# The last down matrix of a decoder step in two column halves, with residual rows added on TensorE

## The chip, the cores and the metric

The kernel runs on one core of a Trainium2 chip. The metric is the device time of one execution in microseconds. A core has TensorE (matrix products into PSUM), VectorE, ScalarE, GpSimd, SyncE (which issues DMAs here) and 16 DMA engines. A DMA can also be issued by ScalarE or GpSimd; the issue then stands in that engine's own queue of instructions.

## What is computed

One decoder layer for 256 prompt tokens and 8 x 4 sample tokens, all with the same weights in float32. The change lies in the last sub-layer, the mixture of experts, and in its last expert:

```python
def hier_moe(n, w_group, b_group, w_router, b_router, w_gate, w_up, w_down):
    ...
    y = jnp.zeros_like(xf)
    for e in range(N_EXPERTS):
        h = jax.nn.silu(xf @ w_gate[e]) * (xf @ w_up[e])
        y = y + combine[:, e:e + 1] * (h @ w_down[e])
    return y.reshape(B, T, D)
...
    return h + hier_moe(rms_norm(h, norm_ffn), ...)
```

D_MODEL is 2048, EXPERT_FF 512, there are 16 experts, and a token goes to two of them. The model's y is h (the residual rows) plus the experts' weighted rows.

## The kernel before

Tokens are sorted to experts by their number. The first ten experts in that order have a block of 64 rows each, the star expert a block and a strip, and the last five (light ones) strips of 32 rows; two strips of different experts share a block. Should more tokens come to an expert than fit, up to 8 overflow blocks follow in a loop that runs none when there is no overflow (`nov` is 0).

For each expert SyncE streams six lots of 2 MB in the order gate 0, up 0, gate 1, up 1, down 0, down 1 into eight buffers in a ring; a lot waits until the one that held its buffer is used up (`moe_free`). A down lot holds, for each of 128 partitions p, the rows 4p+2q and 4p+2q+1 of the down matrix with all their 2048 columns: one piece of 16 KB per partition.

TensorE does for a light expert: gate and up (`light_gate_up`, `strip_products`, L1275: four matmuls 128x256 side by side in four column strips of the array, first half with lots 0 and 1, second half with lots 2 and 3), then ScalarE's silu (L1890), VectorE's product with up (L2430), a transposition on TensorE (L1320) that ScalarE lays into `hTs` (L1869), then the down products (`light_down`, `strip_down`, L1327): a column strip c of the array computes columns 512c to 512c+511 into PSUM partitions 32c to 32c+31. VectorE and ScalarE copy two strips each into `ysb` (`strip_rows`, L2398 and L1875). In `ysb` the partitions 0 to 63 hold the block's 64 rows with columns 0 to 1023, the partitions 64 to 127 the same rows with columns 1024 to 2047.

Combining multiplies `slot_w` (which row of the block goes to which token, with its weight) by `ysb`. For tokens t (0 and 1: the prompt's 256, 2: the 32 of the sample) and x (0 or 1) a step has two products, one on partitions 0 to 63 for columns 512x and one on partitions 64 to 127 for columns 1024+512x. VectorE adds the PSUM rows to `hx`, which holds the residual rows (L2351, L2354). For earlier blocks these steps lie between the gate products of the next expert (`between`).

At the end, after both down lots of expert 15 (`y_last`), the copies, then four steps `last_combine` (L1335) into all eight PSUM banks, VectorE's six additions (L2465), for the sample tokens four more small products (L1473) once the first addition has freed two banks, and after each addition a store from SyncE (L548). The span ends when all six have landed.

Each matmul in float32 stands in the trace as two records.

## Time and profile before

| what | us |
|---|---|
| median of 3 runs | 1251.08 |
| lowest and highest | 1248.23, 1257.48 |
| the profiled execution | 1253.98 |
| its span on the core | 1252.2 |
| TensorE busy in the span | 1165.5 |
| VectorE busy | 471.4 |
| ScalarE busy | 192.7 |

The profiled execution's own time has 1.8 us around its span. "Busy" is an average over the whole kernel. PE is TensorE's matmul, PEld its weight load, DVE is VectorE, ACT is ScalarE, SP is SyncE; an engine's name with q is its queue or sequencer. "<-" names what the engine waited for.

### The profile page before, as it was taken

The numbers are of one execution on the slowest core, as the hardware profiler recorded it, in microseconds if no ns is written. First come the engines' busy times: TensorE is split into PE (matmuls) and PEld (weight loads), VectorE is DVE, ScalarE is ACT, GpSimd is POOL, SyncE is SP. The second block draws the span as 40 slices with busy tenths as digits, with TensorE's granted clock in tenths as the row PEclk, the third lists the DMA queues.
The fourth block names the chain that finished last, engine by engine and source line by source line (L and its number), as shares of the span: only waits on it lengthen the run. The fifth ranks groups of instructions, "written<-read, shape, count | busy, mean of one in ns | idle before, by whom it ended". The sixth has DMA issues, their size and how long they took to land.

```text
span 1252.2 us, 14135 instructions
## 1 busy us (share of the span) xinstructions
PE 1165.5 (93%) x5878; PEld 569.2 (45%) x5878; DVE 471.4 (38%) x962; ACT 192.7 (15%) x405; POOL 49.7 (4%) x64
## 2 busy tenths in 40 slices
PE   7999999999999998899999899999999998999575
PEld 4334443344444455677777675333333333334222
DVE  5000167069835645011113465233333433235122
ACT  2112232300122233100012431000000000001000
POOL 0002000000000003100000001000000000000000
PEclk9999999899999999999999998999999999989788
DMA  8835532435443338854445617999999999999996
GB/s 285 302 125 144 152 101 87 146 123 179 140 135 101 104 136 333 331 156 135 135 168 201 273 69 310 379 428 426 426 426 428 425 427 426 426 364 429 426 427 239
DMA packets 71230, 327.85 MB, mean 262 GB/s; under 512 B 14109, under 2 KB 17981, under 8 KB 54589
## 3 DMA queue, kind: packets, MB, share of 16 engines
q1 hardware_dynamic: 55152, 282.65, 58.0%
q0 software_dynamic: 8032, 37.23, 8.0%
q10 hardware_dynamic: 7980, 7.05, 2.3%
q8 instruction: 48, 0.79, 0.3%
q14 instruction: 18, 0.14, 0.0%
HBM read 319.04 MB, written 10.49 MB: 263 GB/s over the span
## 4 chain that ended last, share of the span: by engine, by line
PE 78%; DVE 9%; DMA 7%; ACT 3%; ACTq 1%; issue 1%; DVEq 0%; SPq 0%
PE PS L691 20%; PE PS L998 15%; PE PS L1268 13%; PE PS L1350 6%; DMA ring<-in_w_up 5%; PE PS L1231 4%; PE PS L664 3%; PE PS L1275 3%; DVE X L2012 2%; DVE top L2011 2%; PE PS L1327 1%; PE PS L809 1%; DMA ring<-in_cache_mem_v 1%; PE PS L1235 1%; PE PS L1343 1%
## 5 line engine op out<-in xcount | busy, mean ns | idle before, releaser
L691 PE MATMUL PS<-ring,NC 128*128 128x512 f32 x704 | 325.5, 608 | 1.6 <-issue 1.6
L691 PEld LDWEIGHTS PS<-ring,NC 128*128 128x128 f32 x704 | 130.4, 193 | 156.1 <-issue 154.6
L998 PE MATMUL PS<-NC,ring 128*128 128x288 f32 x768 | 189.9, 407 | 1.6 <-issue 0.5
L998 PEld LDWEIGHTS PS<-NC,ring 128*128 128x128 f32 x768 | 144.6, 190 | 42.4 <-issue 2.4
L1268 PE MATMUL PS<-ring,NC 128*64 128x512 f32 x512 | 117.4, 598 | 1.4 <-DVE NC L2365 1.4
L2351 DVE TENSOR_TENSOR X<-X,PS 128x1024 f32<-128x1024 f32 x52 | 63.5, 1221 | 118.7 <-PE PS L1231 118.6
L1268 PEld LDWEIGHTS PS<-ring,NC 128*64 128x64 f32 x512 | 34.2, 136 | 79.4 <-issue 77.8
L1350 PE MATMUL PS<-ring,NC 128*64 128x512 f32 x288 | 67.2, 620 | 0.9 <-ACT NC L1864 0.5
L1231 PE MATMUL PS<-XNN,NC 64*128 64x512 f32 x208 | 59.4, 648 | 1.1 <-DVE XNN L2398 0.6
L1859 ACT ACTIVATE NC<-PS,small 64x512 f32<-64x512 f32 x11 | 7.5, 681 | 312.3 <-PE PS L1268 271.3
L2169 DVE TENSOR_TENSOR X<-X,PS 128x288 f32<-128x288 f32 x16 | 7.3, 454 | 115.0 <-PE PS L998 115.0
L2011 DVE MAX8 top<-X 32x8 f32<-32x1028 f32 (+2 forms) x48 | 44.7, 931 | 1.0
L1268 PE MATMUL PS<-NC 128*64 128x512 f32 x96 | 44.3, 598 | 0.0
L1268 PE MATMUL PS<-XNN,NC 128*64 128x512 f32 x96 | 44.3, 598 | 0.0
L1275 PE MATMUL PS<-ring,mkT 128*32 128x256 f32 x384 | 28.7, 452 | 16.6 <-DMA ring<-in_w_up 16.6
L2012 DVE MATCH_REPLACE8 X<-top,X 32x1028 f32<-32x1028 f32 (+2 forms) x48 | 43.9, 914 | 0.0
L2354 DVE TENSOR_TENSOR X<-X,PS 32x1024 f32<-32x1024 f32 x26 | 31.5, 1210 | 28.0 <-PE PS L1235 27.8
L1350 PEld LDWEIGHTS PS<-ring,NC 128*64 128x64 f32 x288 | 20.6, 143 | 45.1 <-issue 38.9
L664 PE MATMUL PS<-ring,NC 128*32 128x512 f32 x288 | 38.4, 605 | 0.0
L1231 PEld LDWEIGHTS PS<-XNN,NC 64*128 64x128 f32 x208 | 15.9, 187 | 38.7 <-issue 25.2
L2394 DVE COPY XNN<-PS 128x1024 f32<-128x1024 f32 x11 | 13.5, 1225 | 52.9 <-PE PS L1350 41.1
L2038 DVE TENSOR_TENSOR ring<-small,cst 64x256 f32<-64x256 f32 x1 | 0.4, 418 | 85.8 <-ACT small L1591 85.8
(438 smaller groups left out, 1146.2 us busy)
## 6 DMA issues: line engine op xcount, KB each, us to landing
ring<-in_w_gate SPq DMA_DIRECT2D x24, 2048.0 KB, 18.5
ring<-in_w_up SPq DMA_DIRECT2D x24, 2048.0 KB, 22.6
ring<-in_w_down SPq DMA_DIRECT2D x24, 2048.0 KB, 21.8
ring<-in_w_in SPq DMA_DIRECT2D x36, 1024.0 KB, 5.0
ring<-in_w_out SPq DMA_DIRECT2D x16, 1024.0 KB, 5.0
XNN<-in_w_gate SPq DMA_DIRECT2D x8, 2048.0 KB, 19.3
NC<-in_w_up SPq DMA_DIRECT2D x8, 2048.0 KB, 22.4
XNN<-in_w_down SPq DMA_DIRECT2D x4, 2048.0 KB, 18.2
```

Of the source, the lines that this page charges most:

```text
L664: last = mm(acc(n, 2)[32 * k:32 * k + 32, 0:width], lhs[:, 4 * q + k, T:NT], ws[:, k, 0:width], start=st, stop=sp_)
L691: last = mm(acc(n, t)[:, 0:width], lhs[:, kt, t * 128:(t + 1) * 128], slot(m)[:, k, 0:width], start=kt == 0, stop=kt == KT - 1)
L998: last = mm(PS[:, j, 0:NT], slot(m)[:, k, 128 * j:128 * j + 128], src[:, kt, :], start=kt == 0, stop=kt == width * 4 - 1)
L1231: last = mm(PS[:, banks + half, :], slot_w[rows, k, 128 * t:128 * t + 128], ysb[rows, k, 512 * x:512 * x + 512], start=True, stop=True)
L1268: last = mm(PS[64 * half:64 * half + 64, 2, :], x[:, kt % 8, kt // 8, :], weights[half][:, kt % 8, :], start=kt == 0, stop=kt == KT - 1)
L1275: last = mm(PS[32 * c:32 * c + 32, bank, 0:256], x[:, kt % 8, kt // 8, STRIP * sub:STRIP * sub + STRIP], weights[c // 2][:, kt % 8, 256 * ...
L1350: last = mm(PS[64 * half:64 * half + 64, bank + x, :], hT[:, f, :], w[:, f % 2, half * 1024 + x * 512:half * 1024 + x * 512 + 512], start= ...
L2011: own(V.max(best, work))
L2012: own(V.match_replace(work, best, work, TAKEN))
L2351: return TT(out, out, PS[:, banks:banks + 2, :], ALU.add)
L2354: last = TT(out, out, PS[32 * x:32 * x + 32, banks:banks + 2, :], ALU.add)
L2394: V.tensor_copy(ysb[:, p % 2, :], PSF[:, 2048:3072]).then_inc(S("y_out_psum"), 1)
```

## The change

- The two down lots of the last expert are loaded by column: lot `part` holds all four rows 4p to 4p+3 of each partition with the columns 1024*part to 1024*part+1023, in four pieces of 4 KB.
- `last_down(half)` computes the 1024 columns of a half in four column strips of 256, with all four row groups f. Strips 0 and 1 are copied by VectorE, 2 and 3 by ScalarE. `last_combine(half)` then multiplies the 64 partitions of that half alone: token tiles 0 and 1 for two x, and the sample tokens in two column strips.
- Prompt tile 0 is added by VectorE as before, in pieces of 128x512. For prompt tile 1 and the sample the residual rows are put into PSUM first, by a product of the identity with `hx`, and the combining product is added onto them. ScalarE copies tile 1 from PSUM into `hx` and issues its stores; VectorE copies the sample's bank into `y_last_s`, which is stored by four small DMAs.
- The residual rows of tile 1 for half 0 are put in early, within the gate products of the last expert; those for half 1 and the sample's between the first down half and its combining.
- Stores: tile 0 in two halves from SyncE, tile 1 in two halves from ScalarE, the sample in four pieces from SyncE.

```diff
--- before.py
+++ after.py
@@ -379,6 +379,7 @@
         NRING = len(ring_at)
         gate_v, up_v = (w[0].rearrange("e (h p k) n -> e p h (k n)", h=2, p=128) for w in (w_gate, w_up))
         down_v = w_down[0].rearrange("e (p k) n -> e p (k n)", p=128)
+        down_cols = w_down[0].rearrange("e (p k) n -> e p k n", p=128)
 
         LOTS = [(w, h) for h in range(2) for w in (gate_v, up_v)] + [(down_v, q) for q in range(2)]
         NL = len(LOTS)
@@ -395,6 +396,7 @@
         hT = C_[:, 3584:3840].rearrange("p (f r) -> p f r", f=4)
         hTs = C_[:, 4416:4416 + 4 * STRIP].rearrange("p (f r) -> p f r", f=4)
         sg_star, hid_star = SQ[:, 0:256], SQ[:, 256:512]
+        y_last_s = SQ[:, 512:1024]
         ysb = XN[:, 0:2048].rearrange("p (b x) -> p b x", b=2)
         tabS = sb("tabS", NBLK, U32)
         tabF = small[:, 256:256 + 3 * NBLK]
@@ -407,7 +409,7 @@
         KEYS_WITH_Q = 9
         TOKENS = (0, 128, NT - 128)
         ROW0 = NBK * CAP
-        LAST = [(t, x) for t in range(3) for x in range(2)]
+        LAST_COMB, COMB_T1, COMB_S, COMB_T0B, COMB_T1B = 5, 2, 3, 4, 5
 
         def sub_of(p):
 
@@ -531,7 +533,11 @@
                         sp.wait_ge(S("n_out"), 48)
                     if lot == 7:
                         sp.wait_ge(S("xg_in0"), 16)
-                    sp.dma_start(ring_at[lot % NRING], lot_of(wv, expert, part)).then_inc(S(f"moe_in{lot % NRING}"), 16)
+                    out, source = ring_at[lot % NRING], lot_of(wv, expert, part)
+                    if e == NEXP - 1 and wv is down_v:
+                        out = out.rearrange("p (k n) -> p k n", k=4)
+                        source = down_cols[expert, :, :, 1024 * part:1024 * part + 1024]
+                    sp.dma_start(out, source).then_inc(S(f"moe_in{lot % NRING}"), 16)
 
             sp.wait_ge(S("route_ready"), 1)
             nov = sp.value_load(ids_nov, min_val=0, max_val=NOVF)
@@ -542,13 +548,16 @@
                     for i, (wv, part) in enumerate(LOTS):
                         sp.wait_ge(S("moe_free"), b * NL + (FREED - NL + i + 1))
                         sp.dma_start(ring_at[SPARE[i]], lot_of(wv, e, part)).then_inc(S(f"moe_in{SPARE[i]}"), 16)
-            for n, (t, x) in enumerate(LAST):
-                sp.wait_ge(S("y_ready"), n + 1)
-                y, row = (y_prompt, t * 128) if t < 2 else (y_sample, 0)
-                sp.dma_start(bass.AP(y.tensor, row * D + 512 * x, [[D, ROWS[t]], [1024, 2], [1, 512]]),
-                             hx[0:ROWS[t], t, :].rearrange("p (h x c) -> p h x c", h=2, x=2)[:, :, x, :])\
+            for half in range(2):
+                sp.wait_ge(S("y_ready"), 2 * half + 2)
+                if half:
+                    for c in range(4):
+                        sp.dma_start(bass.AP(y_sample.tensor, 512 * c, [[D, R], [1, 512]]), y_last_s[32 * c:32 * c + 32, :])\
+                            .then_inc(S("y_stored"), 16)
+                    sp.wait_ge(S("y_ready"), 5)
+                sp.dma_start(y_prompt[0, 0:128, 1024 * half:1024 * half + 1024], hx[:, 0, 1024 * half:1024 * half + 1024])\
                     .then_inc(S("y_stored"), 16)
-            sp.wait_ge(S("y_stored"), 16 * len(LAST))
+            sp.wait_ge(S("y_stored"), 16 * 8)
 
 
         @block.gpsimd
@@ -1328,13 +1337,45 @@
                               start=f == 0, stop=f == 3)
                 return last
 
-            def last_combine(t, x, banks):
-
-                for half in range(2):
-                    rows = slice(64 * half, 64 * half + 64)
-                    last = mm(PS[0:ROWS[t], banks + half, :], slot_w[rows, (NBK - 1) % 2, t * 128:t * 128 + ROWS[t]],
-                              ysb[rows, (NBK - 1) % 2, 512 * x:512 * x + 512], start=True, stop=True)
-                last.then_inc(S("last_comb"), 1)
+            def residual(out, t, col, opens=True):
+
+                rows = slice(0, ROWS[t])
+                mm(out, ident[rows, rows], hx[rows, t, col:col + 512], start=opens, stop=not opens)
+
+            def last_residuals(half, opens=True):
+
+                for x in range(2):
+                    residual(PS[:, 2 * half + x, :], 1, 1024 * half + 512 * x, opens)
+
+            def sample_residuals():
+
+                for c in range(4):
+                    residual(PS[32 * c:32 * c + 32, 4, :], 2, 512 * c)
+
+            def last_down(half, w):
+
+                for f in range(4):
+                    for c in range(4):
+                        last = mm(PS[32 * c:32 * c + 32, 5, 0:256], hTs[:, f, :], w[:, f, 256 * c:256 * c + 256],
+                                  start=f == 0, stop=f == 3)
+                last.then_inc(S("y_last"), 1)
+
+            def last_combine(half):
+
+                rows, k = slice(64 * half, 64 * half + 64), (NBK - 1) % 2
+
+                def product(out, tokens, x, opens):
+                    return mm(out, slot_w[rows, k, tokens], ysb[rows, k, 512 * x:512 * x + 512], start=opens, stop=True)
+                for x in range(2):
+                    if half:
+                        pe.wait_ge(S("y_ready"), x + 1)
+                    product(PS[:, 6 + x, :], slice(0, 128), x, True).then_inc(S("last_comb"), 1)
+                    product(PS[:, 2 * half + x, :], slice(128, T), x, False).then_inc(S("last_comb"), 1)
+                    if x == 0:
+                        for z in range(2):
+                            c = 2 * half + z
+                            last = product(PS[32 * c:32 * c + 32, 4, :], slice(T, NT), z, False)
+                        last.then_inc(S("last_comb"), 1)
 
             def hidden_t(bank=3):
 
@@ -1425,8 +1466,13 @@
                 b, sub = block_of(p), sub_of(p)
                 pe.wait_ge(S("xt_laid"), b + 1)
                 if sub:
-                    light_gate_up((XT, XT2)[(b - PSTAR) % 2], 1, lots_at(p),
-                                  lambda s: combine_step(PSTAR, s) if p == PSTAR + 1 and s < 4 else None)
+                    def between(s):
+                        if p == PSTAR + 1 and s < 4:
+                            combine_step(PSTAR, s)
+                        if p == NEXP - 1 and s == 0:
+                            pe.wait_ge(S("comb_free"), NCOMB_IN)
+                            last_residuals(0)
+                    light_gate_up((XT, XT2)[(b - PSTAR) % 2], 1, lots_at(p), between)
                     pe.wait_ge(S("y_strips"), 2 * (p - PSTAR))
                     if b + 1 < NBK:
                         block_rows_t(b + 1)
@@ -1441,6 +1487,7 @@
                     pe.wait_ge(S("comb_free"), NCOMB_IN)
                     nov = pe.value_load(ids_nov, min_val=0, max_val=NOVF)
                     with pe.If(nov > 0):
+                        last_residuals(0, False)
                         with pe.Fori(0, NOVF) as o:
                             with pe.If(o < nov):
                                 def landed(i):
@@ -1458,21 +1505,18 @@
                                 for s in range(NCOMB_OV):
                                     combine_over(o, s)
                                 pe.wait_ge(S("comb_free"), o * NCOMB_OV + (NCOMB_IN + NCOMB_OV))
+                        last_residuals(0)
                 pe.wait_ge(S("ht_laid"), p + 2)
                 if p < NEXP - 1:
                     light_down(4 + sub, lots_at(p), lambda last, q: last.then_inc(S("moe_free"), 1))
-                else:
-                    light_down(4 + sub, lots_at(p), lambda last, q: last.then_inc(S("y_last"), 1))
-            pe.wait_ge(S("y_strips"), 2 * (NLIGHT + 1))
-            for n, (t, x) in enumerate(LAST[:4]):
-                last_combine(t, x, 2 * n)
-            pe.wait_ge(S("y_ready"), 1)
             for half in range(2):
-                rows = slice(64 * half, 64 * half + 64)
-                for x in range(2):
-                    last = mm(PS[32 * x:32 * x + 32, half, :], slot_w[rows, (NBK - 1) % 2, T:NT],
-                              ysb[rows, (NBK - 1) % 2, 512 * x:512 * x + 512], start=True, stop=True)
-            last.then_inc(S("last_comb"), 1)
+                w = lots_at(NEXP - 1)(4 + half).rearrange("p (f n) -> p f n", f=4)
+                last_down(half, w)
+                if half == 0:
+                    sample_residuals()
+                    last_residuals(1)
+                pe.wait_ge(S("y_strips"), 2 * (NLIGHT + 1 + half))
+                last_combine(half)
 
 
         @block.scalar
@@ -1902,8 +1946,18 @@
                     A(sg[64:128, :], PS[0:64, 2, :], ACT.Silu, scale=over_rs[0:64, :]).then_inc(S("ov_silu"), 1)
                     act.wait_ge(S("ov_ht"), b + 1)
                     A(hT, PS[:, 2, 0:256].rearrange("p (f r) -> p f r", f=4), ACT.Copy).then_inc(S("ov_ht_laid"), 1)
-            act.wait_ge(S("y_last"), 2)
-            strip_rows(NBK - 1, 1, 5)
+            for half in range(2):
+                rows, k = slice(64 * half + STRIP, 64 * half + 2 * STRIP), (NBK - 1) % 2
+                act.wait_ge(S("y_last"), half + 1)
+                for c in (2, 3):
+                    last = A(ysb[rows, k, 256 * c:256 * c + 256], PS[32 * c:32 * c + 32, 5, 0:256], ACT.Copy)
+                last.then_inc(S("y_strips"), 1)
+                for x in range(2):
+                    act.wait_ge(S("last_comb"), LAST_COMB * half + (COMB_T1, COMB_T1B)[x])
+                    col = 1024 * half + 512 * x
+                    own(A(hx[:, 1, col:col + 512], PS[:, 2 * half + x, :], ACT.Copy))
+                act.dma_start(y_prompt[0, 128:T, 1024 * half:1024 * half + 1024], hx[:, 1, 1024 * half:1024 * half + 1024])\
+                    .then_inc(S("y_stored"), 16)
             for name, count in stored:
                 act.wait_ge(S(name), count)
 
@@ -2456,13 +2510,19 @@
                             out = hx[0:R, 2, :].rearrange("p (h x c) -> p h x c", h=2, x=2)[:, :, s - 4, :]
                             last = TT(out, out, PS[96:128, 6:8, :], ALU.add)
                         last.then_inc(S("comb_free"), 1)
-            dve.wait_ge(S("y_last"), 2)
-            strip_rows(NBK - 1, 1, 5)
-            for n, (t, x) in enumerate(LAST):
-                dve.wait_ge(S("last_comb"), min(n, 4) + 1)
-                out = hx[0:ROWS[t], t, :].rearrange("p (h x c) -> p h x c", h=2, x=2)[:, :, x, :]
-                rows = PS[:, 2 * n:2 * n + 2, :] if t < 2 else PS[32 * x:32 * x + 32, 0:2, :]
-                TT(out, out, rows, ALU.add).then_inc(S("y_ready"), 1)
+            for half in range(2):
+                rows, k = slice(64 * half + STRIP, 64 * half + 2 * STRIP), (NBK - 1) % 2
+                dve.wait_ge(S("y_last"), half + 1)
+                for c in range(2):
+                    last = V.tensor_copy(ysb[rows, k, 256 * c:256 * c + 256], PS[32 * c:32 * c + 32, 5, 0:256])
+                last.then_inc(S("y_strips"), 1)
+                for x in range(2):
+                    dve.wait_ge(S("last_comb"), LAST_COMB * half + (1, COMB_T0B)[x])
+                    out = hx[:, 0, 1024 * half + 512 * x:1024 * half + 512 * x + 512]
+                    TT(out, out, PS[:, 6 + x, :], ALU.add).then_inc(S("y_ready"), 1)
+                    if half and x == 0:
+                        dve.wait_ge(S("last_comb"), LAST_COMB + COMB_S)
+                        V.tensor_copy(y_last_s, PS[:, 4, :]).then_inc(S("y_ready"), 1)
 
 
 _INS = ['x_prompt', 'x_sample', 'cache_k', 'cache_v', 'cache_idx_k', 'cache_mem_k', 'cache_mem_v', 'page_table',
```

## Rows read from the trace of the kernel before

**Rows 1.** The page, busy time of each engine: us, share of span, instructions.

```profile
PE 1165.5 (93%) x5878; PEld 569.2 (45%) x5878; DVE 471.4 (38%) x962; ACT 192.7 (15%) x405; POOL 49.7 (4%) x64
```

**Rows 2.** Chain of waits, end of the span: start us, us, what.

```profile
1193.79 30.79 DMA ring<-in_w_up
...
1224.71 6.25 PE PS L1275 x64
...
1233.87 5.06 PE PS L1327 x32
...
1238.95 0.68 DVE XNN L2398
...
1240.39 1.15 PE PS L1335 x4
...
1241.56 4.61 DVE X L2465 x4
```

**Rows 3.** Busy time by engine in stretches; the last three: granted clock, DMA share, GB/s.

```profile
1220.90:1223.00 2.10, 0.00 (x0) 0.00 (x0) 0.00 (x0) 0.00 (x0) 0.00 (x0) 1.00 1.01 429
1224.70:1229.90 5.20, 5.18 (x52) 2.85 (x56) 0.00 (x0) 0.00 (x0) 0.00 (x0) 0.50 1.00 419
1224.70:1233.30 8.60, 7.33 (x80) 4.27 (x80) 0.49 (x1) 0.47 (x1) 0.00 (x0) 0.70 0.93 392
1233.30:1236.70 3.40, 2.83 (x16) 0.92 (x20) 0.00 (x0) 0.28 (x1) 0.00 (x0) 0.50 0.03 10
1240.40:1245.10 4.70, 4.68 (x24) 1.60 (x24) 3.54 (x4) 0.00 (x0) 0.00 (x0) 1.00 0.21 78
1245.10:1250.30 5.20, 0.00 (x0) 0.00 (x0) 3.41 (x3) 0.00 (x0) 0.00 (x0) 1.00 1.01 365
```

**Rows 4.** Timeline, combining products at the end: start us, us, engine, line, records.

```profile
1240.39 3.70 PE L1335 MATMUL PS<-XNN,NC 64*128 64x512 f32 x16 [1.50 <-DVE XNN L2398]
```

**Rows 5.** Timeline, products of one row group, indexer stage (L809).

```profile
237.12 1.90 PE L809 MATMUL PS<-XNN,ring 64*32 64x512 f32 x4
238.86 0.20 PE L809 MATMUL PS<-small,ring 64*32 64x4 f32 x2
...
242.94 3.18 PE L809 MATMUL PS<-XNN,ring 64*32 64x512 f32 x4
```

**Rows 6.** Timeline, products of the identity with 512 columns (L1211).

```profile
753.93 7.11 PE L1211 MATMUL PS<-cst 128*128 128x512 f32 x16
```

**Rows 7.** Timeline, strip and pair products in turn, gate stage.

```profile
1189.21 1.50 PE L1275 MATMUL PS<-ring,mkT 128*32 128x256 f32 x24
1190.64 1.13 PE L1231 MATMUL PS<-XNN,NC 64*128 64x512 f32 x4
1191.70 1.50 PE L1275 MATMUL PS<-ring,mkT 128*32 128x256 f32 x24
```

**Rows 8.** Groups by line and shape: busy us, mean ns, idle before.

```profile
L2351 DVE TENSOR_TENSOR X<-X,PS 128x1024 f32<-128x1024 f32 x4 | 4.9, 1222 | 13.8 <-PE PS L1231 13.8
L1695 ACT ACTIVATE NC<-PS 128x512 f32<-128x512 f32 x8 | 4.8, 597 | 0.8 <-PE PS L891 0.4
L2127 DVE COPY ring<-PS 128x512 f32<-128x512 f32 x8 | 5.3, 679 | 0.7 <-PE PS L944 0.7
```

**Rows 9.** An issue of a down lot; a stretch of the input projection.

```profile
1200.24 0.33 SPq L534 DMA_DIRECT2D XNN<-in_w_down  x1
...
10.00:30.00 20.00, 19.09 (x88) 12.00 (x87) 13.89 (x36) 4.29 (x10) 0.00 (x0) 1.00 0.95 316
```

**Rows 10.** The stores, line 548: issue ns, first and last start; landing.

```profile
L548 SPq DMA_DIRECT2D out<-X x6: 533/572/670, 1242.8 to 1248.6; - x6
...
DMA to landing us min/median/max: 3.2/3.5/4.0
```

**Rows 11.** Busy time in stretches without products, in earlier experts.

```profile
1159.60:1165.00 5.40, 0.27 (x8) 0.00 (x0) 0.00 (x0) 0.00 (x0) 0.00 (x0) 1.00 1.02 434
1179.10:1182.00 2.90, 0.00 (x0) 0.00 (x0) 1.36 (x2) 1.18 (x2) 0.00 (x0) 1.00 1.02 435
```

## The prediction

> **What bounds the kernel now.** I read the page first. TensorE is busy 93% of the span, VectorE 38%, ScalarE 15% [rows 1]. That is an average over all stages and says little about the last 60 us, which are all that the change touches. There I read the chain of waits [rows 2]. For 30.79 us it is the weight stream: the up matrix of the last expert lands at 1224.6, whatever the engines do. From there on it is a chain of single steps: second half of gate and up (6.25), ScalarE, VectorE, transposes, last down products (from 1233.87, 5.06), two copies of strips in a row on each engine (the first 0.68), the first pair of combining products (1.15), then VectorE's additions from 1241.56, 4.61 for four of them and as much each for the other two. Each lets SyncE issue a store; the last issue starts at 1248.6 [rows 10] and the span ends at 1252.2, so 3.6 us are the last store. Third, the busy time in stretches [rows 3]: the stream is over by about 1234 (10 GB/s after 1233.3), and TensorE's granted clock is at half (1.2 GHz) in two stretches that lie on the chain, 1224.7 to 1229.9 and 1233.3 to 1236.7. So the tail from 1224.6 is latency; 7.0 us of it (1241.6 to 1248.6) are additions on VectorE, and TensorE ends its work at 1245.1, 7 us ahead of the end.
>
> **Edit 1, combining products by column half.** Before, the 64 rows of column half 0 and the 64 rows of half 1 are multiplied as a pair: 16 records (two per matmul, so 8 matmuls of 64x512) take 3.70 us [rows 4]. Without some 0.2 us for the end of the last, that is 0.86 for a pair, 0.43 for one. After, all products of one half use the same 64 rows, so there is no partner. The nearest row for products on the same rows is line 809: 4 records, 2 matmuls, of 64x512 in 1.90 us, and the next row starts 1.74 after it, thus 0.86 each [rows 5]. It has 32 output rows and not 128, but the products on 128x128 pace the same: 16 records of 128x512 in 7.11 us, 0.86 a matmul [rows 6]. I take 0.86. A half then costs 5 x 0.86 = 4.3 (t0 and t1 for two x, and the sample pair, which lies side by side in two column strips), both 8.6, against 3.4 + 0.86 before. The bound from below is 0.43 each, if they did overlap: 4.3 for all.
> The Trainium skill, "TensorE: Matmul & The Clock Gate", section "Why this matters for your kernels", says that a single matmul with a small K takes as long as one with K=128 and that all the gain is from tiles running together. The rows agree; this speaks against the change.
>
> **Edit 2, residual rows through TensorE.** The sample rows (4 matmuls 32x512 in four column strips, together 0.86) and two 128x128x512 (2 x 0.86) stand between the first down half and its combining: 2.57 us. The strips' copies run beside it and hide 0.8 of that, no more. The pair for half 0 is put into the gate products at 1215, where TensorE is idle from 1220.9 to 1224.7 [rows 3]: even at 1.2 GHz it takes 3.4 us and fits, in front of a transfer that is not moved. Its new wait is for additions of the block before, which VectorE did over 10 us earlier.
>
> **Edit 3, changes of tile shape.** In the rows where 32-column strips and 64-row pairs alternate, 24 strip records should take 1.28 and the next shape starts 1.43 later; 4 pair records should take 0.86 and the next starts 1.06 later [rows 7]. So a change costs about 0.18. The new tail has six of them up to the second down half and two in the second combining: 1.4 us, where before both lay in idle time. Bounds: 0 and 8 x 0.2.
>
> **Edit 4, ScalarE takes t1, sizes shrink.** An addition of 128x1024 takes 1.22 and VectorE copies 128x512 in 0.68, so an addition of 128x512 lies between 0.61 and about 0.7, I take 0.69; ScalarE copies 128x512 in 0.60. A strip copy of 32x512 takes 0.68 [rows 2, 8], so one of 32x256 lies between half of it, 0.34, and the whole; since each has a fixed part, 0.41. Strip copies for a half: 0.8 on both engines at once. These are each shorter than the 0.86 of the product that feeds them, so they wait on TensorE: VectorE's relief, some 7 us, is real but the wait moves to TensorE.
>
> **Edit 5, loads and stores.** The two last loads have pieces of 4 KB in place of 16 KB. By the stretches, the stream does 425 GB/s (429 at a share of 1.01); in the input projection, with 2 KB pieces, 316 at 0.95, 333 [rows 3, 9]. As a worst case the two lots' 4.2 MB take 12.6 in place of 9.9. Of them 8.6 x 392 KB and little more move after 1224.7, about 3.4 MB, so the first is in at about 1228, or 1229.4 in the worst case; it is used at 1231 at the earliest. The cover is 1.8 us, and the second lot is used 10 us later. Cost 0. Stores: six on SP became four of 128x1024 and four small ones, of which SP must issue the four small ones ahead of its last large one. An issue took 0.33 for loads and 0.57 for the old stores [rows 9, 10], so 1.3 to 2.3 us after the sample copy; ScalarE issues its own; behind that issue for half 0 stand its strip copies of half 1, which start 2 us later by the sum below, so nothing waits. From issue to landing 3.2 to 4.0 us [rows 10]. The last two stores, 512 KB each, now leave together: at the 365 GB/s of the store stretch [rows 3] each adds 1.4 us to the other. Before, the last store was 128 KB, alone.
>
> **The sum, with the clock as before.** First down half from 1233.87: four groups of four strips with 256 columns each, half of 0.86 a group, 1.71 us at full speed; up to 1236.7 the clock is at half, which does 1.42 of it, so it ends at 1237.0. Residuals 2.57 and three changes 0.54: 1240.1 (the strips were ready at 1238.1). First combining 4.3 and two changes: 1244.75; one change and the second down half 1.71: 1246.65, results 0.2 later, copies 0.8: 1247.7. Second combining with its changes and end 4.95: 1252.7. ScalarE's copy: 1253.3. Store 3.6 + 1.4: 1258.3. Against 1252.2 that is +6.1.
> **What the clock gives back.** Before, TensorE idles from 1220.9 and the clock falls at 1223, 1.7 us ahead of the next work. The residual pair moves the end of that work to 1222.2 (3.4 at the slow level, of which the later strips regain part at the fast one). Elsewhere the clock held for 5.4 and for 2.9 us after the last product [rows 11], and for 2.1 in this one; the idle time is now 2.5. So it more likely than not stays at 2.4 GHz, and the second gate half takes 3.6 in place of 6.25: -2.6. All later steps move with it, and the slow stretch at 1233.3 costs less or falls elsewhere: 0 to -1.4, I take -0.4. Net +6.1 - 3.0 = +3.1 us. The profiled execution of before ran 1253.98 with its span at 1252.2, and the median is 1251.08; I add the difference to the median: 1254.2.
>
> **Rivals and chances.** A change of 1% is 12.5 us, about what a measurement of this kernel can tell from none.
> - Forecast: TensorE becomes the bound of the tail, the clock gives half of it back: 1254.2, own range 1252 to 1256. Chance 0.48.
> - The same without the clock's gift: 1257.2, up to 1259 with 0.57 for each issue and landings at 4.0. 0.30.
> - VectorE's relief reaches the end: products on the same rows overlap after all, -4.3 on the forecast: 1249.9. For it: each is half an array. Against it: line 809. 0.10.
> - Other side, slower: the clock falls during the unpaired products and stays down. At line 809 it fell at 243.4 in the middle of such products (4 records in 3.18 us in place of 1.90) [rows 5]. All 12 us of TensorE work after 1237 would take twice as long: 1257.2 + 12 = 1269. Against it: there the stretch ahead had idle gaps, here it is dense. It would leave the 1% band if 6.4 of those 12 us ran slow. 0.05.
> - The last loads are late by more than the 1.8 us of cover, or something else that I do not see: 0.07.
> Range 1248.5 to 1260.5 leaves out the slower case and part of the unseen. Faster by over 1%: 0.02; within 1%: 0.92; slower by over 1%: 0.06.
>
> **What the profile of the changed kernel would show.** The combining products as 0.86 us each, with VectorE and ScalarE idle between their additions on TensorE's account; TensorE near busy from the first down half to some 4 us ahead of the end; the second gate half in 3.6 us at a granted clock of 1.00 (or 6.2 at 0.50 to 0.56, the second case); the last large stores landing 4 to 5 us after issue. I am wrong if products of one half overlap (0.43), if the residuals hide behind the copies, or if the last additions end before 1248.

## The result

The changed kernel is slower, by 0.66% (ratio 1.0066, interval 1.0042 to 1.009; medians 1262.91 against 1252.79, 7 executions each). The medians lie 10.1 us apart; the ratio, which I go by, gives 8.3. Run again it was 0.54% (1.0025 to 1.0084; 12 against 26 executions). I had said +3.1 us, or 1254.2 with a range up to 1260.5; it is +8.3 and +6.8 us. So the sign and "within 1%" were right, the size was not: more than half of the loss was missing, and 1262.91 lies above the range.

Executions of either kernel scatter over some 15 us, and a span goes with the time that TensorE spends at the lower clock. Write L = 2 x (1 - mean granted clock) x span: the time at the lower level, since that is half of the upper one. Over 108 executions of before the span rises by 0.39 us for each us of L. I therefore give for each kernel the mean L and the rest, span - 0.39 L, with one standard error. (The span is 1.8 us shorter than the time.) The standard error of a mean L is 2 to 4 us, for before 0.8, so a difference in L of less than some 8 us is not clear of the scatter.

| kernel | mean us (executions) | ratio to before, interval | mean L | rest |
|---|---|---|---|---|
| before | 1252.9 (108) | | 79.0 | 1220.3 ± 0.1 |
| changed | 1260.8 (7) | 1.0066, 1.0042 to 1.009 | 80.6 | 1227.6 ± 0.5 |
| changed, again | 1259.3 (12) | 1.0054, 1.0025 to 1.0084 | 77.2 | 1227.4 ± 0.6 |

The whole loss is in the rest, +7.2; the time at the lower clock has not changed on the mean (-0.3 ± 2.5 us for the 19 executions together). One execution of after_nojump below, 1267.19 us, is counted as slow and left out; with it that run's mean is 1256.8.

The chain of waits of the changed kernel, from the last weights that set it (start us, us, what):

```profile
1190.32 29.49 DMA ring<-in_w_up
...
1219.95 5.41 PE PS L1284 x64
...
1228.19 2.78 PE PS L1359 x21
1230.96 0.14 issue
1231.11 1.12 PE PS L1359 x11
1232.23 2.90 PE PS L1343 x12
1235.13 4.80 PE PS L1368 x12
1239.93 1.91 PE PS L1359 x32
...
1242.77 7.34 PE PS L1368 x12
...
1250.19 0.60 ACT X L1958
```

Line 1284 is the gate products (1275 before), 1359 a down half, 1343 the residual products, 1368 the combining products. Where rows 2 had VectorE's additions, there are now only TensorE's products and one copy of ScalarE. From the landing of the up matrix (1219.81) to the end of the span (1253.8) it is 34.0 us, against 27.6 in [rows 2]. I call this stretch the tail. This execution's span is only 1.6 us longer since its stream ended 4.8 us earlier. The second combining takes 7.34 where the first takes 4.80, and the stretches tell why (granted clock third from the end):

```profile
1219.95:1221.00 1.05, 1.05 (x20) 0.78 (x24) 0.00 (x0) 0.00 (x0) 0.00 (x0) 1.00 1.03 414
1221.00:1222.00 1.00, 1.00 (x19) 0.66 (x12) 0.00 (x0) 0.00 (x0) 0.00 (x0) 0.52 1.03 410
...
1235.00:1240.00 5.00, 5.00 (x17) 1.62 (x20) 1.38 (x2) 0.60 (x1) 0.00 (x0) 1.00 0.00 0
...
1244.70:1245.70 1.00, 1.00 (x5) 0.12 (x4) 0.00 (x0) 0.60 (x1) 0.00 (x0) 0.62 0.00 0
1246.70:1247.70 1.00, 1.00 (x2) 0.44 (x2) 0.42 (x1) 0.00 (x0) 0.00 (x0) 0.50 0.00 0
```

The clock falls near 1245, in the middle of unpaired products, as it falls at 1221 in the middle of the gate half. The two large stores of ScalarE, against [rows 10]:

```profile
L1959 ACTq DMA_DIRECT2D out<-X x2: 338/358/377, 1240.7 to 1250.8; - x2
...
DMA to landing us min/median/max: 2.6/2.9/3.1
```

### The profile page after: what moved, and what is told of

Same layout as the page of the kernel before. It is cut to its first block, busy times and chain, and to the rows that moved or that the text cites. A ratio compares the mean times of both kernels' runs of the same rounds, so it can differ in the third digit from the quotient of the medians.

```text
span 1253.8 us, 14242 instructions
## 1 busy us (share of the span) xinstructions
PE 1171.1 (93%) x5926; PEld 571.4 (46%) x5926; DVE 468.2 (37%) x963; ACT 195.2 (16%) x411; POOL 49.7 (4%) x64
## 4 chain that ended last, share of the span: by engine, by line
PE 80%; DVE 8%; DMA 8%; ACT 3%; issue 1%; SPq 0%; DVEq 0%; ACTq 0%
PE PS L700 20%; PE PS L1007 15%; PE PS L1277 13%; PE PS L1391 6%; DMA ring<-in_w_up 5%; PE PS L1240 4%; PE PS L673 3%; PE PS L1284 3%; DVE X L2066 2%; DVE top L2065 2%; PE PS L818 1%; DMA ring<-in_cache_mem_v 1%; PE PS L1244 1%; PE PS L1368 1%; PE PS L1384 1%
## 5 line engine op out<-in xcount | busy, mean ns | idle before, releaser
L700 PE MATMUL PS<-ring,NC 128*128 128x512 f32 x704 | 320.9, 601 | 1.6 <-issue 1.6
L2405 DVE TENSOR_TENSOR X<-X,PS 128x1024 f32<-128x1024 f32 x52 | 63.5, 1221 | 119.1 <-PE PS L1240 119.1
```

The costliest lines, as they stand in the source:

```text
L700: last = mm(acc(n, t)[:, 0:width], lhs[:, kt, t * 128:(t + 1) * 128], slot(m)[:, k, 0:width], start=kt == 0, stop=kt == KT - 1)
L2405: return TT(out, out, PS[:, banks:banks + 2, :], ALU.add)
```

## The experiments

All runs are on the kernel before or the changed one with the edit named.

| run | mean us (executions) | ratio to before, interval | mean L | rest |
|---|---|---|---|---|
| partner | 1260.0 (12) | 1.006, 1.0032 to 1.0088 | 75.9 | 1228.6 ± 0.6 |
| nores | 1263.7 (9) | 1.0077, 1.0045 to 1.0109 | 95.1 | 1224.8 ± 0.6 |
| early | 1266.2 (6) | 1.0109, 1.0071 to 1.0147 | 95.3 | 1227.2 ± 0.3 |
| halves | 1262.1 (6) | 1.0078, 1.0048 to 1.0108 | 91.2 | 1224.7 ± 0.6 |
| after_nojump | 1255.9 (11) | 1.0028, 0.9997 to 1.0058 | 73.9 | 1225.2 ± 0.7 |
| before_nojump | 1253.5 (12) | 1.0006, 0.9986 to 1.0026 | 78.0 | 1221.0 ± 0.4 |
| gapfill | 1251.2 (12) | 0.999, 0.9965 to 1.0015 | 71.5 | 1221.5 ± 0.5 |
| shift52 | 1261.4 (6) | 1.0064, 1.0039 to 1.0089 | 81.9 | 1227.7 ± 0.8 |
| shift116 | 1263.1 (6) | 1.0075, 1.0054 to 1.0096 | 82.0 | 1229.3 ± 0.9 |
| shift188 | 1256.7 (12) | 1.0022, 1.0003 to 1.0042 | 72.2 | 1226.7 ± 0.4 |
| pair_shift | 1257.6 (12) | 1.0035, 1.0015 to 1.0055 | 82.7 | 1223.5 ± 0.4 |
| pair_nojump | 1254.3 (12) | 1.0004, 0.9983 to 1.0024 | 76.4 | 1222.7 ± 0.3 |
| pair_dve | 1254.6 (12) | 1.0011, 0.9993 to 1.0029 | 79.1 | 1221.9 ± 0.7 |
| pair_dve_nojump | 1250.7 (12) | 0.9973, 0.995 to 0.9995 | 73.1 | 1220.4 ± 0.5 |
| rowlots | 1262.8 (7) | 1.0061, 1.0031 to 1.0091 | 85.8 | 1227.6 ± 1.1 |
| best | 1251.7 (12) | 1.0, 0.998 to 1.0019 | 72.5 | 1221.6 ± 0.3 |

### The changed kernel again

No edit.

> The changed kernel once more, on the chip of the next three, as their yardstick. The tail is counted from the landing of the last expert's up matrix (the end of the long DMA step in the chain of waits) to the end of the span: 27.6 us before, 34.0 in the first profile of the changed kernel. Theory (the loss is all in the tail, on TensorE): a tail of 33 to 36 us, with each combining half 4.7 to 4.8 us at a granted clock of 1.00 and up to 9 at 0.50, and a time of 6 to 9 us over before. Rival (the time of the first profile, only 1.7 us over that of before, is the true one and the medians are noise): within 3 us of before.

The tail is 34.5 us, and the second profile shows a new thing (chain of waits):

```profile
1219.64 3.72 PE PS L1284 x64
...
1226.21 1.49 PE PS L1359 x21
1227.70 2.06 issue
1229.77 1.05 PE PS L1359 x11
1230.82 4.56 PE PS L1343 x12
1235.38 4.80 PE PS L1368 x12
...
1243.01 7.22 PE PS L1368 x12
```

Here the second gate half ran at full clock (3.72), and the first down half stood still for 2.06 us in its middle, after 21 of 32 records, with nothing that it waited for. It would have stood so in the first profile too, but there the 21 records ran slow (2.78) and only 0.14 was left. The residual products (4.56) then ran slow. Part of what the clock gave was taken back by a stall that my sum doesn't have.

At 1229.63 the second down lot landed in this profile, so one might take the stall for a wait on it. It is not: the first half doesn't read that lot, and in the profile of the next run TensorE went on at 1230.41 while the lot landed at 1230.44.

### A partner for each product

```diff
+                other = slice(64 - 64 * half, 128 - 64 * half)
...
                 def product(out, tokens, x, opens):
+                    if tokens.stop - tokens.start == 128:
+                        mm(PS[:, 5, :], slot_w[other, k, tokens], ysb[other, k, 512 * x:512 * x + 512],
+                           start=True, stop=True)
                     return mm(out, slot_w[rows, k, tokens], ysb[rows, k, 512 * x:512 * x + 512], start=opens, stop=True)
```

> Each 128-column combining product gets a partner on the other 64 rows, into a PSUM bank that is free (its values are not used). Theory A (a product on 64 rows leaves the other half of the array empty): the partners are free, each combining half still takes 4.7 to 4.9 us at full clock. Rival A' (products on other rows don't run beside it): each half takes 3.4 us more, the tail 7 us more. Theory B (the clock fell in the second combining half since only half of the rows worked): with partners it stays at 1.00 there, the second half takes 4.8 in place of 7.3, tail about 31.5. Rival B' (it fell because of the wait for the strips' copies and the moment at which it came): the partners change nothing, the clock falls here too, tail 33 to 36.

Timeline (L1371 the partner, L1373 the product):

```profile
1236.48 0.59 PE L1371 MATMUL PS<-XNN,NC 64*128 64x512 f32 x1
1236.49 0.59 PE L1373 MATMUL PS<-XNN,NC 64*128 64x512 f32 x1
1236.91 0.59 PE L1371 MATMUL PS<-XNN,NC 64*128 64x512 f32 x1
```

Partners start 0.01 us beside their products and a record still starts each 0.43: they are free, so half of the array had been empty. Theory A holds. The clock stayed at 1.00 through the second combining (4.9 us, tail 33.7 with the stall), as B wants, but L over 12 executions is 75.9 against 77.2 and 80.6, too near to tell. Nor does the one profile tell: the second combining ran at full clock without partners too, 4.88 us in after_nojump, shift116, shift188, nores and early below. B stays open.

### No residual products

```diff
             def residual(out, t, col, opens=True):
-                mm(out, ident[rows, rows], hx[rows, t, col:col + 512], start=opens, stop=not opens)
+                return
...
```

The combining products then open their banks themselves.

> No residual products: prompt tile 1 and the sample are stored without their residual rows. Theory (they stand on the path between the first down half and its combining): the first combining half starts at the end of the strips' copies, 0.9 us after the first down half, not 2.9; with the end of the copies counted that is a gain of 2.0 us, tail 32, less what the clock takes back in the gate products, where the pair for half 0 is gone too (up to 1 us). Rival (they are hidden behind the strips' copies): gain under 0.5 us.

The work went (rest 2.7 below the changed kernel), but TensorE was 15 to 18 us longer at the lower clock, and the time rose by 3.8 ± 1.7 us. Timeline: the first down half and the first combining, slow, and ScalarE's first strip copy.

```profile
1239.57 3.42 PE L1359 MATMUL PS<-XNN,NC 128*32 128x256 f32 x32 [0.45 <-ACT NC L1913]
1243.49 0.77 ACT L1953 ACTIVATE XNN<-PS 32x256 f32<-32x256 f32 x2 [4.05 <-PE PS L1359]
1244.31 7.64 PE L1368 MATMUL PS<-XNN,NC 64*128 64x512 f32 x12 [1.32 <-ACT XNN L1953]
```

So the residual products were not hidden (theory), and yet taking them out costs, which neither side had said. The copy of ScalarE ends the wait here: its overflow loop, which finds nothing, keeps it for 4.05 us after it has laid the hidden rows. Before, the down products (5.06 in [rows 2]) covered that. This run takes out the pair in the gate stage too, whose hold on the clock was in my sum, so it doesn't say which of the residual products hold it.

### All residual products early

```diff
                             last_residuals(0)
+                            last_residuals(1)
+                            pe.wait_ge(S("y_strips"), 2 * (p - PSTAR))
+                            sample_residuals()
...
-                if half == 0:
-                    sample_residuals()
-                    last_residuals(1)
...
```

> All residual products moved into the gate products of the last expert, where TensorE waits for the stream; tile 0 uses the banks 2 and 3 in place of 6 and 7. Theory: the 2.9 us between first down half and combining shrink to the 0.9 of the copies, and the fuller gap keeps the clock at 1.00 in the second gate half: 3.6 us there, tail 30.5 to 32. Rival (the added 4.3 us of products, 8.6 at the lower clock, are longer than the gap): the second gate half starts 1 to 4 us after the up matrix has landed and the gain is eaten, tail 33 to 35.

Worse than either side said: 1.1% over before.

```profile
1229.27 3.64 PE L1359 MATMUL PS<-XNN,NC 128*32 128x256 f32 x32 [3.46 <-issue]
1233.87 9.33 PE L1368 MATMUL PS<-XNN,NC 64*128 64x512 f32 x12 [0.96 <-DVE XNN L2521]
```

The stall is now ahead of the first down product, 3.46 us with what the copy before it takes, and the clock then fell for the first down half and the first combining (9.33 in place of 4.8). The second gate half did run at full clock, as the theory has it, but the tail is 38.7 us.

### Without the overflow code, in both kernels

In TensorE's program the block `with pe.If(nov > 0):` is left out, so overflow blocks would not be computed; there are none with these inputs.

> The changed kernel without TensorE's code for overflow blocks (none occur for these inputs; the kernel would be wrong for inputs that have one). In two profiles TensorE stands still for 2.06 us in the middle of the first down half, after 21 records, and in the kernel with early residuals for 3.1 us ahead of it, with nothing to wait for; in the first profile the gap at the same record was 0.14, with the records before it slow. Theory F (the jump over the overflow code makes TensorE wait for its next instructions until some 4 us after the transposition): without the jump the first down half takes 1.9 us at full clock with no gap, and the span is 1.5 to 2.5 us shorter at equal time at the lower clock. Rival F' (the stall is something else, a semaphore or the arrival of the down lot): the gap is there again and the time is the same.

> The kernel before without TensorE's code for overflow blocks, as the control for the run ahead. Its profile has no gap in the down products (32 records of 512 columns, the first ones slow). Theory F: the instructions come in time here since the products ahead of the page's end take longer; same time as before within 1 us. Rival: the jump costs as much here, 2 us less.

```profile
1229.69 1.93 PE L1359 MATMUL PS<-XNN,NC 128*32 128x256 f32 x32 [0.57 <-ACT NC L1892]
...
1233.48 0.77 ACT L1932 ACTIVATE XNN<-PS 32x256 f32<-32x256 f32 x2 [4.05 <-issue]
1234.45 4.87 PE L1368 MATMUL PS<-XNN,NC 64*128 64x512 f32 x12
...
1242.16 4.87 PE L1368 MATMUL PS<-XNN,NC 64*128 64x512 f32 x12 [0.97 <-DVE XNN L2496]
```

The stall is gone (32 records in 1.93), both combinings run at full clock, and the tail is 29.3 us. Against the mean of the changed kernel's 19 executions the gain is 4.0 ± 1.8 us, of it 2.2 ± 0.8 in the rest; that L is less (4.5 ± 4.4) isn't shown. The second down lot landed at 1233.09, after the first half was done: it is not waited for. The kernel before gains nothing (1.0006). So the stall comes with the overflow code (theory F and not F'), and the kernel before doesn't have it.

### Moving the code

```diff
                 b, sub = block_of(p), sub_of(p)
+                if p >= NEXP - 4:
+                    for _ in range(56):   # 25: shift52, 94: shift188
+                        pe.wait_ge(S("xt_laid"), b + 1)
                 pe.wait_ge(S("xt_laid"), b + 1)
```

Two such waits are built into one instruction, so shift116 moves the code by 112, the others by 52 and 188. I counted the built programs, two instructions a record and one a wait; the borders are those at which the stalls of the first profiles stood.

> The changed kernel, whole, with 112 waits more in TensorE's program that are long fulfilled, spread over the last four experts where TensorE waits for the stream. They only move the code behind them. Counted in instructions, the place to which the jump over the overflow code leads then lies 68 past a border of 256 at which the two stalls seen so far stood (44 instructions behind the target in the changed kernel, 28 ahead of it in the one with early residuals), and the jump itself 16 past the border before. Theory F (the code comes in pieces of 256 instructions, the next one only after the jump): no stall, as without the overflow code, 1.5 to 2.5 us less than the changed kernel at equal time at the lower clock. Rival (the stall belongs to the overflow code itself, wherever it stands): 2.06 us again.

> The same with 52 waits more: the target of the jump then lies 8 instructions behind the border, and the jump ahead of the border before it. Theory F: now the target itself isn't there, TensorE stands still for 3 to 3.6 us ahead of the first down product, as with the early residuals, and the time at equal clock is 0.5 to 2 us more than the changed kernel's. Rival (added waits help or do nothing): 2 us or less of a stall.

> The changed kernel whole, with 188 waits more that are long fulfilled. Mended theory F: TensorE's next piece of 256 instructions is there some 4 us after the last one was entered, by running on or by a jump. With 112 more the jump stood only 16 instructions past a border, so the piece behind it was still under way: stall 2.9 us, to 3.5 us after the transposition. With 188 the jump stands 92 past the border, the target 144 past the next and 112 ahead of the one after: no stall ahead of the first down half or in it; the code after that is needed over 4 us later. 1.5 to 2.5 us less than the changed kernel at equal time at the lower clock. Rival (the overflow code stalls wherever it lies): 2 to 4 us ahead of or in the first down half.

First down half in the timelines of shift52, shift116 and shift188, in this order:

```profile
1230.13 3.64 PE L1359 MATMUL PS<-XNN,NC 128*32 128x256 f32 x32 [4.52 <-issue]
```

```profile
1236.61 3.64 PE L1359 MATMUL PS<-XNN,NC 128*32 128x256 f32 x32 [3.45 <-issue]
```

```profile
1234.31 1.93 PE L1359 MATMUL PS<-XNN,NC 128*32 128x256 f32 x32 [0.53 <-ACT NC L1916]
```

The same program with more waits in it stands still for some 4 us, 3 us and not at all. My rule was wrong at first: for shift116, and for pair_shift and pair_dve below, it said no stall. Mended (a piece that has just been entered does not yet have the next one behind it), it foretold shift188, and best below. Against the changed kernel shift188 gains 3.2 ± 1.2 us on the mean, but only 0.8 ± 0.6 of it in the rest, where I had said 1.5 to 2.5. The rival, that the overflow code stalls wherever it lies, is out.

The traces have a second sign. They list a DMA queue under the name "instruction", with pieces of 16 KB. DMA view of after_again, 1226.8 to 1227.4, and of early, 1225.8 to 1227:

```profile
q8 instruction: 1, 0.02, 11.2%
```

```profile
q8 instruction: 1, 0.02, 4.9%
```

In each of the seven profiles in which TensorE stood still (after_again, partner, early, shift52, shift116, pair_shift, pair_dve) one such piece starts 2.5 to 2.8 us before TensorE goes on. In shift188 none starts between the last transposition and the end of the first down half. In before one starts at 1234.4, under down products that go on to 1238.9. Whose instructions they are the profile doesn't say.

### One part alone: the column halves, VectorE adding

```diff
-                    own(A(hx[:, 1, col:col + 512], PS[:, 2 * half + x, :], ACT.Copy))
...
+                    out = hx[:, 1, 1024 * half + 512 * x:1024 * half + 512 * x + 512]
+                    TT(out, out, PS[:, 2 * half + x, :], ALU.add).then_inc(S("y_ready"), 1)
```

and no residual products.

> The column halves alone: no residual products, VectorE adds all rows as in the kernel before, in pieces of 128x512, the store of tile 1 still issued by ScalarE. Compared with the kernel without residual rows and without these additions (nores), which lay 12 us over before, mostly through 18 us more at the lower clock. Theory D (the unpaired products and the clock that falls in them are the loss; residual products and ScalarE's share don't matter much): as nores or 0 to 2 us more, so 10 to 14 us over before. Rival D' (residual products are the loss): within 4 us of before.

9.2 us over before, a little under the 10 to 14 of theory D and far from the 4 of the rival: no ratio below 1.0048 is in the interval. VectorE's additions hide behind the unpaired products (rest as nores). So the halves alone are enough for a loss as large as the whole change's. But it is made otherwise: 4.4 us in the rest and 12 us more L than before, where the changed kernel has 7.2 and none. The residual products with ScalarE's share cost 2.8 in the rest and save 13 us of L: in time the two are 2.2 ± 1.5 us apart, which isn't clear of the scatter.

### The part that helps before

```diff
+                        if p == NEXP - 1 and s == 0:
+                            pe.wait_ge(S("comb_free"), NCOMB_IN)
+                            for x in range(2):
+                                mm(PS[:, x, :], ident, hx[:, 1, 512 * x:512 * x + 512], start=True, stop=True)
...
```

> The kernel before with one addition: two products of the identity with 512 columns, of no use, among the gate products of the last expert, where the changed kernel puts its first residual pair. Theory C (they hold the clock through the wait for the up matrix): the second gate half at 1.00, 3.7 us in place of 6.25 in most executions, 1 to 2.6 us less in time, mean granted clock up. Rival C' (the clock falls as often as before, only at another moment): no gain within 1 us, mean clock unchanged.

```profile
1213.17 3.66 PE L1275 MATMUL PS<-ring,mkT 128*32 128x256 f32 x64 [1.98 <-DMA ring<-in_w_up]
...
1222.84 1.92 PE L1327 MATMUL PS<-NC 128*32 128x512 f32 x16 [1.21 <-DMA NC<-in_w_down]
```

The second gate half took 3.66 (6.25 in [rows 2]) and a part of that went at once: the second down lot is now late by 1.21. The time is 0.999 (0.9965 to 1.0015) and L is 7.5 ± 3.9 us below before, so neither a gain nor less time at the lower clock is shown; and this profile is of the fastest of the 12 executions (1239.86). What speaks for the clock's answer is all the profiles together: with two products in that wait the second gate half took 3.7 us in nine and 5.4 in five, without them 6.2 to 6.3 in three and 5.4 in one (before_nojump). (In early, with more products, it ran at full clock.)

### Pairs at the end

All rows of both halves are combined in pairs after the second down half; ScalarE's tile 1 starts then.

```diff
-                    product(PS[:, 6 + x, :], slice(0, 128), x, True).then_inc(S("last_comb"), 1)
+                    for h in range(2):
+                        last = product(h, PS[:, 2 + h, :], slice(0, 128), x, True)
```

> Residual products and ScalarE's share as in the change, down matrix in column halves and strips copied by half, but the combining products as pairs of both halves at the end, and the code moved as in the first run of this batch. Theory A (unpaired products cost 4.3 us): combining 5 x 0.86 in place of 10 x 0.86 and one wait for copies less; down halves 3.6, residuals 2.9 over the copies, combining and its changes 4.7, VectorE's last addition 1.2, store 4.4: from the start of the first down half to the end 17 to 18 us at full clock, against 22.5 in the kernel without the jump; time 0 to 4 us below before. Rival (the loss is in the residual products and stores): 20 us or more, time above before.

> The kernel with pairs of both halves at the end (residual products and ScalarE's share kept), without TensorE's overflow code. With that code it stood still for 4.6 us ahead of the first down half. Theory A (unpaired products are the loss beside the stall): from the start of the first down half to the end 17 to 18 us at full clock against 22.5 without pairs; at equal time at the lower clock 4 to 5 us below the changed kernel without overflow code, so about 1220 to 1221.5 in span less 0.39 of the lower clock's time (1220.2 before). Rival (the stall only hid another wait): above 1223.

pair_shift stood still for 4.6 us ahead of the first down half, so it can't tell. Without the stall the rest is 1222.7, 2.5 ± 0.7 below after_nojump, where I said 4 to 5: between the theory's 1221.5 and the rival's 1223. The products did as they should; SyncE is what is late next:

```profile
1238.81 4.90 PE L1370 MATMUL PS<-XNN,NC 64*128 64x512 f32 x24
...
1243.44 3.52 SPq L555 DMA_DIRECT2D out<-SQ  x4
1243.83 1.22 DVE L2510 TENSOR_TENSOR X<-X,PS 128x1024 f32<-128x1024 f32 x1 [0.42 <-PE PS L1370]
...
1247.00 0.59 SPq L558 DMA_DIRECT2D out<-X  x1
```

All combining products in 4.90, VectorE is done at 1245.05, but the four small stores hold SyncE until 1247, and the last large store leaves 1.9 us late.

```diff
-            dve.wait_ge(S("y_last"), 2)
-            strip_rows(NBK - 1, 1, 5)
+            for half in range(2):
+                rows, k = slice(64 * half + STRIP, 64 * half + 2 * STRIP), (NBK - 1) % 2
+                dve.wait_ge(S("y_last"), half + 1)
...
```

is the edit of the next three (with the column lots and the early products), additions and stores as before:

> The kernel before with three things only: the two useless products that hold the clock in the gate stage, the last down matrix in column halves with the strips of a half copied at once, and the code moved. Pairs, additions and stores as before. Theory: against the run with the two products alone, the wait of 1.2 us for the second down lot goes (a lot of columns is needed later) and the strips' copies of the first half hide, 0.5: from the first down product to the end 16.5 to 17 us at full clock in place of 18.3, time 1 to 4 us below before. Rival (the column pieces slow the loads, or the shorter products lose the clock): no less than before.

> The kernel before with the two useless products in the gate stage and the down matrix in column halves, pairs, additions on VectorE, without TensorE's overflow code. Against the run ahead it tells what residual products and ScalarE's share are worth when nothing stalls. Theory: VectorE's 7 us of additions are the path here, from the first down product to the end 17 us at full clock; residual products with ScalarE the same within 1 us, since they add 2.9 us of products and take off some 3.5 of additions. Rival (the shared additions pay): this one 2 us or more above the run ahead.

> The kernel before, whole, with the two useless products in the gate stage, the down matrix in column halves, strips copied by half, and the code moved by 188 waits so that the jump stands 92 instructions past a border and its target 128 ahead of the next. Theory F as mended: no stall (in the same kernel moved by 112 it was 2.0 us), and the time as without overflow code, 1 to 4 us below before. Rival: a stall of 2 us or more in or ahead of the first down half, and the time of before or above.

pair_dve stalled for 2.0 us. Without the overflow code it is the only run ahead of before, 0.9973 (0.995 to 0.9995); among so many runs an interval that ends that near to 1 is weak. It lies 3.6 ± 1.0 us below pair_nojump, where the theory had them within 1 us and the rival had it 2 us above: with pairs, the residual products and ScalarE's share, with their stores, cost time. The whole kernel, code moved, had no stall but came out at 1.0 (0.998 to 1.0019): not below before as I had expected, and 1 us above the version without overflow code, whose own gain is therefore small at best. First down half of pair_dve_nojump (the second stands under it), then of best, which ran it at the lower clock:

```profile
1234.43 1.93 PE L1461 MATMUL PS<-XNN,NC 128*32 128x256 f32 x32 [0.57 <-ACT NC L1867]
...
1237.88 1.93 PE L1461 MATMUL PS<-NC 128*32 128x256 f32 x32 [1.51 <-DMA NC<-in_w_down]
```

```profile
1231.75 3.45 PE L1483 MATMUL PS<-XNN,NC 128*32 128x256 f32 x32 [0.54 <-ACT NC L1889]
```

### The last lots by rows

```diff
-                    if e == NEXP - 1 and wv is down_v:
-                        out = out.rearrange("p (k n) -> p k n", k=4)
-                        source = down_cols[expert, :, :, 1024 * part:1024 * part + 1024]
```

> The changed kernel with the last two down lots loaded by rows as before (16 KB pieces); each half takes its columns from both lots, so the first half waits for both. Theory (the loads are hidden): the first down half waits up to 1.5 us for the second lot in executions with the clock up, else none; time within 1.5 us of the changed kernel at equal clock. Rival (the pieces of 4 KB cost): 2 us or more less than the changed kernel.

The first half waited longer than I said:

```profile
1235.59 1.93 PE L1356 MATMUL PS<-XNN,NC 128*32 128x256 f32 x16 [3.73 <-DMA NC<-in_w_down]
```

The rest is that of the changed kernel, but this wait lies over the time in which that one stalls, so the comparison doesn't price the pieces. The landings do: the two down lots land 4.9 and 9.8 us after the up matrix here and 4.9 and 10.0 in before, and 5.1 and 10.1 in the changed kernel. Pieces of 4 KB cost 0.1 to 0.4 us, which nothing in the changed kernel waits for.

### Step by step without the stall

Four kernels lead from the changed one back, in the rest: changed 1227.5 (19 executions), without TensorE's overflow code 1225.2, with pairs 1222.7, with VectorE adding all rows and without residual products 1220.4, against 1220.3 of before. The steps, taken before rounding, are 2.2 ± 0.8, 2.5 ± 0.7 and 2.3 ± 0.6. So the loss of 7.2 is in near equal parts the stall, the unpaired products, and the residual products with ScalarE's share and the stores. (The last kernel keeps the column halves and has the two useless products in the gate stage. The runs stand on different chips, but the rest of before is 1220.1 to 1220.4 on each.)

## Why the prediction was wrong, step by step

**What bounds the tail (right in kind).** A latency chain from the landing of the up matrix. My forecast is a tail of 27.6 + 3.1 = 30.7 us; it is 34.0 and 34.5. In the first profile the second gate half took 5.41 where I had 3.6, the first down half 4.0 for 2.7, the second combining 7.34 for 4.95, and the end after ScalarE's last copy 3.0 for 5.0. In the second it is the first down half with its stall, 4.6 for 2.7, the residual products, 4.56 for 3.1, the second combining, 7.22 for 4.95, and the end, 3.1 for 5.0. So two steps failed: that the clock, once held, stays, and a stall that I had at nothing. The store term, too large, hid some 2 us of them.

**Edits 1, 3, 4 (right).** Unpaired products at 0.86 us each: a combining half with its changes of shape measures 4.80 to 4.88, I had 4.65 and 4.95 with the end. Partners are free. At full clock (after_nojump) VectorE and ScalarE waited 1.2 to 2.4 us for TensorE ahead of each addition or copy of rows, but for VectorE's last (0.35). From the first down product to the end, all at full clock: 22.5 us in after_nojump, 18.3 in gapfill, so with the clock held in both the change costs 4.2 us there, stall apart.

**Edit 2 (right in size, half of it missing).** 2.90 us where I had 3.1. I had reckoned that the pair in the gate stage holds the clock. Without any residual product L is 11 to 18 us more than with them (halves, nores), more than that one stretch of 6 us can give; which products do it stays open.

**Edit 5 (loads right, store term too large).** The first down lot lands 5.1 us after the up matrix (I had about 3.4) and is used 6.7 us after it at the earliest. For the stores I had 5.0 from ScalarE's last copy to the end; it is 3.0 in the first profile and 4.5 in after_nojump. In the first the slow clock had drawn the two last stores apart (1249.14 and 1250.82), in the second they leave together (1247.68 and 1247.76).

**The term that wasn't there: a stall of TensorE for its instructions.** The sum took the chain after the last transposition as in [rows 2], with 0.27 us ahead of the down products. The change makes the code ahead of and in the overflow block longer, so the jump leads to a place 44 instructions ahead of a border in place of 68, and the down half shorter, so that they are used up in 1.5 us. It measures 2.06 us where the clock is up and 0.14 in the first profile, where it was down; taking it away is worth 3.2 ± 1.2 (shift188) to 4.0 ± 1.8 us (after_nojump). The Trainium skill, "Runtime: NRT & Kernel Launch", section "Instruction fetch mechanics", says that code comes in blocks of 256 instructions ahead of use, and that a taken branch to a place outside the loaded ones makes the engine wait. The three shifts agree with it, with 0 to some 4 us for it. The diff shows that a block that is jumped over gets longer; where it then lies only a count of the built program tells.

**What the clock gives back (wrong).** I took -3.0. The gift in the gate half is there (3.72 and 5.41 for 6.25, though before_nojump, without the pair, had 5.41 too), but the clock falls again later: in the second combining (7.34 and 7.22 for 4.88), 2.4 us each time, in the second profile in the residual products as well. L is on the mean what it was. That is the slower rival in small: I gave it all 12 us or nothing, where it takes a part of one combining half. So the forecast was the wrong one of my two first cases: "the same without the clock's gift", 1257.2, is what the clock did on the mean. That its +6.1 and the stall of 2.06 add up to 8.2, near the measured 8.3, is partly luck: the second run gives 6.8, and the store term in it is 0.5 to 2 us too large.

**The range.** The median that I added to (1251.08 of 3) is 1.7 below that of 7 executions; +8.3 on it would be 1259.4, inside. The range did not allow for that, nor for the stall.

## What to carry to other kernels

Cutting a stage in halves to finish each early pays only if the halves don't share the array: here the two halves were each other's partners, and 4.3 us of products came back for 7 us of additions that then waited for them. Removed products can cost more than they took, by the clock (nores: 2.7 us less in the rest, 3.8 more in time), so count both levels for each stretch of the new tail. And where the changed code lies by a jump, look for idle time with no releaser: the same program moved by 136 instructions (shift52, shift188) was 4.7 ± 1.4 us faster.

## What the hardware showed that I had not expected

- A jump over some 300 instructions of TensorE's program made it wait up to some 4.5 us, by where it lay: resumed 4.1 us after the last transposition in after_again, 3.5 in early and shift116, 4.5 in shift52, 5.1 in pair_shift, 2.6 in pair_dve; no wait in shift188 and best.
- A loop of eight passes that finds nothing to do keeps ScalarE 4.05 us and VectorE 4.72 (after_nojump, shift188). In nores and halves it is on the path, where the combining waits 1.32 us for ScalarE's copy.
- The clock fell in the midst of work: at 1221.0 one us into the gate half, and near 1245 in unpaired products. Whether unpaired products make it fall is open: the second combining ran slow in after, after_again, shift52 and rowlots (6.9 to 7.4 us) and at full clock, without partners, in six other profiles (4.88), and the partners' mean L doesn't decide.
